# Heads' states multiplied turned round in a hybrid decoder layer's mixer: ScalarE copies them, VectorE's work per head in another order

## The chip, the cores and the metric

The kernel runs on one core of a Trainium2 chip, in float32 for nearly everything. The metric is the device time in microseconds of one execution, as the median over several runs. The engines are TensorE (PE, with its weight loads PEld), VectorE (DVE), ScalarE (ACT), GpSimd (POOL) and SyncE (SP), which here only issues transfers.

## The reference

One inference step of a decoder layer over 512 prompt tokens and 8 samples, width 1024: a mixer with a pooling part and an mLSTM part of 4 heads (128 wide), cross attention into 256 memory tokens, and a two-level mixture of 16 experts. The change lies in the mLSTM part. With no earlier state the prompt's heads come down to this, for each head:

```python
s   = einsum('bhjd,bhsd->bhjs', q, k) * w_intra          # causal scores
num = einsum('bhjs,bhsv->bhjv', s, v)
qn  = s.sum(-1)
h   = num / maximum(abs(qn), exp(-m_t))[..., None]
C_new = einsum('bhs,bhsv,bhsd->bhvd', w_state, v, k)     # an output, v rows by k columns
n_new = einsum('bhs,bhsd->bhd', w_state, k)              # an output
hn  = (h - mean(h)) * rsqrt(var(h) + eps)                # then times sigmoid(og) and a gain
```

The pooling part takes trailing means over 2, 4, 8 and 16 tokens minus the token itself, and multiplies each of its four channel groups by a 128 x 128 matrix. Both parts together go through one output projection.

## The kernel before

All five engines have an instruction list of their own, written out by hand; they meet through semaphores only. PSUM has two rings of three banks: one that ScalarE empties (`bank_a` on TensorE, `full` on ScalarE, counted by `act_full` and `act_free`) and one that VectorE empties (`bank_d`, `dve_full`, `dve_free`). A bank of a ring can be written again when the bank three before it in the ring's order has been taken.

Around the change TensorE does, for each head h of 0 to 3: `scores(h)` (four matmuls of 512, 384, 256 and 128 columns, L658, one bank each, and four transposes of the keys into a fifth bank, L663), then half of a projection (two channel blocks of `og` or `u`, L477, on ScalarE's ring), the transposes of the previous head (`transpose_heads`, L692), `numerators(h)` (ten matmuls of 129 columns, the 129th a column of ones that gives the sum, L673, ScalarE's ring), `state(h)` (L682 and L684) and the next head's scores. After `state(3)` come eight convolution matmuls of the pooling groups in the order 2, 3, 1, 0, each waiting for VectorE's `pool_diff` of its group (L738), then the first token tile's output projection (L774), in the midst of which stand the transposes of head 3.

VectorE does, for each head, `head_norm1(h)` (the denominator, the scaling of the numerators, `bn_stats` and `bn_aggr`), `take_state(h)` (two copies into `Cout`, L1910 and L1911), `products(h+1)` (scores times weights, L1877, and the keys times their state weights into `kw`, L1880), then work for the samples (`carried`, L1948), and `head_norm2(h)` (minus mean, times root, L1936). For head 2 `head_norm2` follows `products(3)` at once, and then come `pool_diff(2)`, `carried(4)`, `pool_diff(3)`, `carried(5)`, `take_heads(2)`, `take_last(0)`, `pool_diff(1)`, `pool_diff(0)` and `head_norm1(3)`. `pool_diff(0)` needs GpSimd's `window_sums`.

ScalarE copies the numerators (L1443) and then computes the next head's weights (`weights`, exponentials, L1434 and L1435), which the products need.

GpSimd takes the root of the variance (`head_rstd(h)`, which `head_norm2(h)` waits for), masks the products on the diagonal blocks (`masks(h)`, which `numerators(h)` waits for), brings the samples' states forward (`load_state`, `update_state`, each of these behind a `carried` of VectorE), and issues the states' stores (`state_out`).

`kw` and `Cout` lie in `gb`, the place of the norm vectors; the ln1 vectors are loaded there when all states are stored.

Of the kernel before, what the change touches and what calls it, by code (L numbers as in the profile page):

```python
# [18 lines left out]
ALU = mybir.AluOpType  # L19
ACT = mybir.ActivationFunctionType  # L20
# [106 lines left out]
def layer_kernel(nc, a, o):  # L127
# [3 lines left out]
    with ctx:  # L131
# [104 lines left out]
        kw = gb[:, 0, 0:512].rearrange("p (t k) -> p t k", t=NQT)  # L236
        Cout = gb[:, 1, 0:512].rearrange("p (b k) -> p b k", b=2)

# [93 lines left out]
        c_in = [sem(f"c_in{i}") for i in range(2)]  # L332
        c_store = [sem(f"c_store{i}") for i in range(2)]
        hs_var, hs_rstd = sem("hs_var"), sem("hs_rstd")
        sq2_out, kq_done = sem("sq2_out"), sem("kq_done")
# [113 lines left out]
        def _(pe):  # L449
# [227 lines left out]
            def state(h):  # L677

                pe.wait_ge(dve_free, at["keys", h])
                bk = bank_d()  # L680
                for i in range(NQT):
                    mm(bk[:, 0:HD], vn[:, i, h, 0:HD], kw[:, i, :], start=(i == 0), stop=(i == NQT - 1))  # L682
                for i in range(NQT):
                    last = mm(bk[0:1, HD:2 * HD], vn[:, i, h, HD:HD + 1], kw[:, i, :], start=(i == 0), stop=(i == NQT - 1))  # L684
                last.then_inc(dve_full, 1)
                at["state", h] = nd[0]

# [26 lines left out]
            at["og", 1] = na[0]  # L714
            transpose_heads(0)
            numerators(1)
            state(1)
# [3 lines left out]
            transpose_heads(1)  # L721
            transpose_last(1)
            numerators(2)
            state(2)
# [4 lines left out]
            at["heads", 2] = nd[0]  # L729
            transpose_last(0)  # L730
            numerators(3)
            state(3)
# [45 lines left out]
            for name, bk in zip(WO, banks):  # L778
                w = wring[:, BI[name] % WR]
                mm(bk[0:TR, :], mixT[:, KC - 1, 0:TR], w[:, KC - 1, :], start=False, stop=True).then_inc(dve_full, 1)  # L780
            rows_project(1, WO, mixT)
            transpose_x(0, x1_ready)
# [395 lines left out]
        def _(sp):  # L1178
# [41 lines left out]

            sp.wait_ge(act_full, at["pool"])
            for n in range(2):
                kv_load(n)
# [102 lines left out]
        def _(act):  # L1326
# [111 lines left out]
            def take_numerators(h):  # L1438
                if h >= 2:
                    act.wait_ge(dve_full, at["heads", h - 2])  # L1440
                for j in range(NQT):
                    bk = full()
                    A(hn[:, h % 2, j, :], bk[:, 0:HD + 1], ACT.Copy).then_inc(act_free, 1)  # L1443

            def take_og(cts):

                for ct in cts:
                    for c0, cn in GRP:
                        bk = full()
                        A(sgT[:, ct, c0:c0 + cn], bk[:, 0:cn], ACT.Exp, scale=-1.0).then_inc(act_free, 1)  # L1450
# [12 lines left out]
            take_og((0, 1))  # L1463
            take_numerators(0)
            weights(1)
            finish_og((0, 1))
            take_og((2, 3))
            take_numerators(1)
            weights(2)
            finish_og((2, 3))  # L1470
            take_projection(uT, (2, 3), 1.0, off=PADC)
            take_numerators(2)
            weights(3)
            take_projection(uT, (0, 1), 1.0, off=PADC)
            take_numerators(3)
            act.wait_ge(c_store[0], 16 * BUF.count(0))
            for g in (2, 3, 1, 0):
# [3 lines left out]
            def take_sample_rows(dstn):  # L1481
# [3 lines left out]
                last.then_inc(act_free, 1)  # L1485

            for t in range(3):
                take_x(t)
# [187 lines left out]
        def _(dve):  # L1676
# [228 lines left out]

            def take_state(h):
                bk = full()
                if h >= 2:
                    dve.wait_ge(c_out[h % 2], 32)
                V.tensor_copy(Cout[:, h % 2, 0:HD], bk[:, 0:HD])  # L1910
                V.tensor_copy(Cout[0:1, h % 2, HD:2 * HD], bk[0:1, HD:2 * HD]).then_inc(dve_free, 1)  # L1911

            def head_norm1(h):

                dve.wait_ge(act_free, at["numerators", h])
                x = hn[:, h % 2]
                qn = x[:, :, HD:HD + 1].rearrange("p t c -> p (t c)")
                d0 = den[:, 0, :]
                link(V.scalar_tensor_tensor(d0, qn, -1.0, qn, ALU.mult, ALU.max))
                fl = gcol[:, 16 + h:32:4]  # L1920
                link(V.tensor_tensor(d0, d0, fl, ALU.max))
                link(V.reciprocal(d0, d0))
                link(V.tensor_tensor(x[:, :, 0:HD], x[:, :, 0:HD], d0.unsqueeze(2).broadcast_to([128, NQT, HD]), ALU.mult))
                for t in range(NQT):
                    last = V.bn_stats(hst[:, t, :], x[:, t, 0:HD])
                link(last)
                for t in range(NQT):
                    last = V.bn_aggr(hagg[:, t, :], hst[:, t, :])
                last.then_inc(hs_var, 1)

            def head_norm2(h):
                dve.wait_ge(hs_rstd, h + 1)
                dve.wait_ge(hs_var, h + 1)
                for t in range(NQT):
                    x = hn[:, h % 2, t, 0:HD]
                    last = V.tensor_scalar(x, x, hagg[:, t, 0:1], den[:, 1, t:t + 1], ALU.subtract, ALU.mult)  # L1936
                last.then_inc(hn_ready, 1)
# [35 lines left out]

            head_norm1(0)
            take_state(0)
            products(1)
            carried(0)
            carried(1)
            head_norm2(0)
            take_heads(0)  # L1980
            head_norm1(1)
            take_state(1)
            products(2)
            carried(2)
            carried(3)
# [3 lines left out]
            head_norm1(2)  # L1989
            take_state(2)  # L1990
            products(3)
            head_norm2(2)
            pool_diff(2)
# [7 lines left out]
            head_norm1(3)  # L2001
            take_state(3)
            head_norm2(3)
# [465 lines left out]
        def _(pool):  # L2469
# [69 lines left out]
            def state_out(h):  # L2539
                pool.wait_ge(dve_free, at["state", h])  # L2540
                pool.dma_start(o_pC[0, 0, h], Cout[:, h % 2, 0:HD]).then_inc(c_out[h % 2], 16)
                pool.dma_start(o_pn[0, 0, h:h + 1], Cout[0:1, h % 2, HD:2 * HD]).then_inc(c_out[h % 2], 16)

# [59 lines left out]
            for h in (0, 1):  # L2603
# [3 lines left out]
                load_state(2 * h + 3)  # L2607
                state_out(h)
                head_rstd(h + 1, TR, NQT)
                masks(h + 2)  # L2610
            state_out(2)
            update_state(4)
            update_state(5)
            window_sums()
            load_state(6)
            head_rstd(3, TR, NQT)
            state_out(3)
            update_state(6)

            def norm_vectors(gname, bname):  # L2620
                pool.dma_start(gb[:, 0, :], a[gname][0].partition_broadcast(128)).then_inc(gb_in, 16)
                pool.dma_start(gb[:, 1, :], a[bname][0].partition_broadcast(128)).then_inc(gb_in, 16)


            for i in range(2):
                pool.wait_ge(c_out[i], 64)
            norm_vectors("ln1_g", "ln1_b")
            load_state(7)
# [3 lines left out]
            pool.dma_start(o_spool[0, :, 0:NPOOL - 1, :], a["cache_pool"][0, :, 1:NPOOL, :]).then_inc(un_out, 16)  # L2632
            norm_rstd(0)
            update_state(7)
            norm_rstd(1)
# [146 lines left out]
```

## Time and profile before

| what | value |
|---|---|
| median of 3 runs | 669.05 us (668.71 to 669.43) |
| profiled execution, its own time | 672.56 us |
| its span in the trace | 670.8 us |
| TensorE busy | 639.7 us (95%) |
| VectorE busy | 348.3 us (52%) |
| ScalarE busy | 151.8 us (23%) |
| GpSimd busy | 208.7 us (31%) |
| TensorE's part of the chain that ended last | 86% |

Times in the rows are microseconds from the span's start. In a timeline, equal neighbours are merged (x4 is four instructions), and the bracket at the end gives the idle time of the engine before them and what ended it. A float32 matmul leaves two records. "PE ps L682 x8" is eight records of line 682 writing PSUM. The line numbers are those of the kernel before.

### The profile page before, as it was taken

To read this page: it belongs to the slowest core of one execution; us is meant where nothing else is said; L and a number is where in the kernel's file an instruction comes from. 1 tells how busy PE (TensorE), PEld (TensorE's weight loads), DVE (VectorE), ACT (ScalarE), POOL (GpSimd) and SP (SyncE) were. 2 spreads that over 40 slices of the span, in tenths; PEclk is the share of its full clock that TensorE was granted. 3 is DMA by queue.
4 is the path that set the end of the run, shared out by engine and by line. 5 is a ranking of instruction groups with operands and counts; after the bars stand their busy time and mean duration, and the time that the engine had idled before them with its cause. 6 is when DMAs were issued, how large, how long until landed. Compare 5 with 4: busy or idle time off the path is not lost.

```text
span 670.8 us, 8667 instructions
## 1 busy us (share of the span) xinstructions
PE 639.7 (95%) x3244; PEld 392.0 (58%) x3244; DVE 348.3 (52%) x799; ACT 151.8 (23%) x333; POOL 208.7 (31%) x245
## 2 busy tenths in 40 slices
PE   6999999999999999999999899999899999999982
PEld 3445588887788774446888674444574454333330
DVE  0283356327456883757643856356863334253445
ACT  1113311102533230002002540223224111111144
POOL 4241010101566565412000985102344422111331
PEclk9999999999999999999999899999989999999996
DMA  8994478703353354004706777554539999999598
GB/s 301 391 319 165 142 172 225 250 20 126 99 171 116 102 201 149 17 0 148 291 0 245 256 268 301 220 178 168 235 124 385 410 414 404 373 354 412 196 204 161
DMA packets 45811, 146.14 MB, mean 218 GB/s; under 512 B 5738, under 2 KB 6058, under 8 KB 41663
## 3 DMA queue, kind: packets, MB, share of 16 engines
q1 hardware_dynamic: 31559, 107.50, 42.6%
q0 software_dynamic: 12032, 33.29, 17.6%
q10 hardware_dynamic: 2176, 4.76, 1.9%
q8 instruction: 27, 0.44, 0.3%
q14 instruction: 17, 0.14, 0.1%
HBM read 130.34 MB, written 20.33 MB: 225 GB/s over the span
## 4 chain that ended last, share of the span: by engine, by line
PE 86%; DMA 7%; DVE 2%; ACT 2%; POOL 1%; issue 1%; ACTq 0%; DVEq 0%; POOLq 0%
PE ps L602 14%; PE ps L749 13%; PE ps L1089 12%; PE ps L511 9%; PE ps L477 8%; PE ps L1109 5%; PE ps L600 4%; DMA xn<-y_d 3%; PE ps L850 2%; PE ps L774 2%; PE ps L976 2%; PE ps L658 2%; PE ps L1070 1%; PE ps L673 1%; PE ps L539 1%
## 5 line engine op out<-in xcount | busy, mean ns | idle before, releaser
L749 PE MATMUL ps<-wring,P 128*128 128x512 f32 x224 | 99.2, 596 | 0.0
L749 PEld LDWEIGHTS ps<-wring,P 128*128 128x128 f32 x224 | 41.6, 190 | 49.1 <-issue 49.0
L1089 PE MATMUL ps<-wring,P 128*32 128x512 f32 (+1 forms) x288 | 66.3, 604 | 0.9 <-DVE P L2344 0.9
L1768 DVE SCALAR_TENSOR_TENSOR P<-ps,P 128x264 f32<-128x264 f32 (+1 forms) x70 | 28.8, 426 | 61.0 <-PE ps L602 44.4
L511 PE MATMUL ps<-wring,P 128*128 128x512 f32 x128 | 58.2, 613 | 1.0 <-DVE P L1723 0.8
L477 PE MATMUL ps<-xT,wring 128*128 128x312 f32 (+1 forms) x256 | 56.8, 383 | 0.0
L2505 POOL TENSOR_SCALAR rstd<-agg 128x1 f32<-128x1 f32 (+1 forms) x15 | 16.8, 1120 | 113.5 <-DVE agg L1708 113.4
L477 PEld LDWEIGHTS ps<-xT,wring 128*128 128x128 f32 x256 | 46.6, 190 | 9.3
L2344 DVE COPY P<-ps 128x512 f32<-128x512 f32 x11 | 7.6, 691 | 76.7 <-PE ps L1070 71.2
L1089 PEld LDWEIGHTS ps<-wring,P 128*32 128x32 f32 (+1 forms) x288 | 22.6, 131 | 36.8 <-issue 36.8
L511 PEld LDWEIGHTS ps<-wring,P 128*128 128x128 f32 x128 | 24.7, 196 | 31.3 <-issue 31.0
L2650 POOL TENSOR_TENSOR P<-P,xT 128x2048 f32<-128x2048 f32 x8 | 36.0, 4520 | 11.9 <-DMA xT<-sq_d 9.1
L1109 PE MATMUL ps<-P 128*32 128x512 f32 (+1 forms) x144 | 32.6, 594 | 0.7 <-issue 0.7
L2020 DVE SCALAR_TENSOR_TENSOR xn<-xn,ps 128x512 f32<-128x512 f32 x16 | 10.9, 684 | 40.1 <-PE ps L749 28.1
L1368 ACT ACTIVATE xT<-ps 128x512 f32<-128x512 f32 (+1 forms) x30 | 13.9, 519 | 75.4 <-PE ps L539 75.2
L602 PE MATMUL ps<-xT,wring 128*128 128x264 f32 (+1 forms) x128 | 29.6, 387 | 0.0
L602 PE MATMUL ps<-P 128*128 128x264 f32 x128 | 29.5, 385 | 0.0
L602 PE MATMUL ps<-P,wring 128*128 128x256 f32 (+1 forms) x128 | 29.2, 382 | 0.0
L1089 PE MATMUL ps<-xT,P 128*32 128x512 f32 (+1 forms) x96 | 28.2, 593 | 0.0
L602 PEld LDWEIGHTS ps<-P 128*128 128x128 f32 x128 | 24.3, 190 | 4.2
L602 PEld LDWEIGHTS ps<-xT,wring 128*128 128x128 f32 x128 | 23.8, 190 | 4.8 <-issue 1.1
L602 PEld LDWEIGHTS ps<-P,wring 128*128 128x128 f32 x128 | 24.2, 190 | 3.8
(444 smaller groups left out, 1106.6 us busy)
## 6 DMA issues: line engine op xcount, KB each, us to landing
wring<-in_w_in SPq DMA_DIRECT2D x5, 2048.0 KB, 10.2
wring<-in_w_gate SPq DMA_DIRECT2D x10, 1024.0 KB
wring<-in_w_up SPq DMA_DIRECT2D x10, 1024.0 KB
P<-in_w_down SPq DMA_DIRECT2D x10, 1024.0 KB, 11.7
P<-in_cache_mem_k SPq DMA_DIRECT2D x8, 1024.0 KB, 7.5
P<-in_cache_mem_v SPq DMA_DIRECT2D x8, 1024.0 KB, 4.9
y_d<-P POOLq DMA_DIRECT2D x1, 4160.0 KB, 32.3
wring<-in_ca_wv SPq DMA_DIRECT2D x2, 2048.0 KB, 19.9
```

Source lines behind the costliest of these rows:

```text
L477: last = mm(out, lhs(k), rhs(k), start=(k == 0), stop=(k == n - 1))
L511: last = mm(bk[:, :], memT[:, k, m * 128:m * 128 + 128], w[:, k, :], start=(k == 0), stop=(k == KC - 1))
L600: last = mm(bank[:, 0:n], x[:, k, 128 * i:128 * i + 128], w[:, k, :], start=(k == 0), stop=(k == 3))
L602: last = mm(bank[:, 0:n], w[:, k, 128 * i:128 * i + 128], x[:, k, :], start=(k == 0), stop=(k == 3))
L658: mm(bk[:, 0:NP_ - t * TR], kT[:, h, t * TR:t * TR + TR], qT[:, h, t * TR:NP_], start=True, stop=True).then_inc(dve_full, 1)
L749: last = mm(bk[:, :], src[:, k, START[t]:START[t] + TR], w[:, k, :], start=(k == 0), stop=(k == KC - 1))
L1089: last = mm(GU[p % 2][lo:lo + m, :].rearrange("p (g f) -> p g f", g=2), xgT[:, p % 3, k, lo:lo + m], gu[s][:, :, k, :], start=(k == 0), st ...
L1109: last = mm(YB[q][lo:lo + m, :], hT[:, p % 2, f, lo:lo + m], dn[s][:, f, q * 512:q * 512 + 512], start=(f == 0), stop=(f == 1))
L1368: A(xT[:, 4 * q:4 * q + 4, START[t]:START[t] + n], bk[:, 0:4 * n].rearrange("p (k c) -> p k c", k=4), ACT.Copy).then_inc(act_free, 1)
L1768: V.scalar_tensor_tensor(dst, src, scale, part, ALU.mult, ALU.add).then_inc(part_added, 1)
L2505: link(G.tensor_scalar(x, agg[0:n, 1:2], LN_EPS, None, ALU.add))
L2650: G.tensor_tensor(x, x, qb[:, b % 4:b % 4 + 1].broadcast_to([128, 2, D]), ALU.mult).then_inc(kq_done, 1)
```

## The change

- `state(h)` multiplies with the two operands exchanged. Each of four matmuls has `kw` as the weights and 129 columns of `vn` moving, so the bank holds the state with k on the partitions and v along the columns, and n as column 129. The second group of matmuls, with one row of output for n, is gone. The bank is now of ScalarE's ring.
- ScalarE takes it: `take_state(h)`, one copy of 128 columns and one of one column, behind `take_numerators(h)` and ahead of `weights(h+1)`. TensorE turns the copy back (`transpose_state(h)`, behind `transpose_heads(h)` and `transpose_last`; for head 3 in the output projection), and ScalarE copies the turned state (`take_turned_state(h)`). The places are three column ranges of `qT`, whose head is used up by then. `Cout` is gone.
- On VectorE `take_state` is gone, `head_norm1(h)` ends with the scaling, and the statistics are a step of their own, `head_statistics(h)`, behind `products(h+1)`.
- `head_norm2` uses `scalar_tensor_tensor` with the root broadcast along the columns as third operand, in place of `tensor_scalar` with the root as a second scalar.
- On GpSimd `state_out(h)` waits for ScalarE's turned copy, stands behind `head_rstd(h+1)` and `masks(h+2)`, and stores n as 128 pieces of 4 bytes; `state_out(2)` and `state_out(3)` come later, and the ln1 vectors are loaded earlier, as soon as TensorE has finished `state(3)`. SP waits for the states' stores before it loads the samples' memory keys, since they go over `qT`.

```diff
             def state(h):
                 pe.wait_ge(dve_free, at["keys", h])
-                bk = bank_d()
+                bk = bank_a()
                 for i in range(NQT):
-                    mm(bk[:, 0:HD], vn[:, i, h, 0:HD], kw[:, i, :], start=(i == 0), stop=(i == NQT - 1))
-                for i in range(NQT):
-                    last = mm(bk[0:1, HD:2 * HD], vn[:, i, h, HD:HD + 1], kw[:, i, :], start=(i == 0), stop=(i == NQT - 1))
-                last.then_inc(dve_full, 1)
-                at["state", h] = nd[0]
+                    last = mm(bk[:, 0:HD + 1], kw[:, i, :], vn[:, i, h, :], start=(i == 0), stop=(i == NQT - 1))
+                last.then_inc(act_full, 1)
+                at["state", h] = na[0]
+
+            def transpose_state(h):
+                pe.wait_ge(act_free, at["state", h])
+                nc.tensor.transpose(bank_a()[:, 0:HD], stateT[:, h, :], ident).then_inc(act_full, 1)
+                at["turned state", h] = na[0]
...
+            def take_state(h):
+                bk = full()
+                A(qT[:, h, 0:HD], bk[:, 0:HD], ACT.Copy)
+                A(state_n[:, h, :], bk[:, HD:HD + 1], ACT.Copy).then_inc(act_free, 1)
+
+            def take_turned_state(h):
+                bk = full()
+                A(stateC[:, h, :], bk[:, 0:HD], ACT.Copy).then_inc(act_free, 1)
...
             take_og((2, 3))
+            take_turned_state(0)
             take_numerators(1)
+            take_state(1)
             weights(2)
...
-                link(V.tensor_tensor(x[:, :, 0:HD], x[:, :, 0:HD], d0.unsqueeze(2).broadcast_to([128, NQT, HD]), ALU.mult))
+                V.tensor_tensor(x[:, :, 0:HD], x[:, :, 0:HD], d0.unsqueeze(2).broadcast_to([128, NQT, HD]), ALU.mult).then_inc(scaled_done, 1)
+
+            def head_statistics(h):
+
+                x = hn[:, h % 2]
+                dve.wait_ge(scaled_done, h + 1)
...
-                    last = V.tensor_scalar(x, x, hagg[:, t, 0:1], den[:, 1, t:t + 1], ALU.subtract, ALU.mult)
+                    last = V.scalar_tensor_tensor(x, x, hagg[:, t, 0:1], den[:, 1, t:t + 1].broadcast_to([128, HD]), ALU.subtract, ALU.mult)
...
             head_norm1(2)
-            take_state(2)
             products(3)
+            head_statistics(2)
             head_norm2(2)
             pool_diff(2)
...
                 load_state(2 * h + 2)
                 load_state(2 * h + 3)
-                state_out(h)
                 head_rstd(h + 1, TR, NQT)
                 masks(h + 2)
-            state_out(2)
+                state_out(h)
...
             window_sums()
+            pool.wait_ge(act_full, at["state", 3])
+            norm_vectors("ln1_g", "ln1_b")
             load_state(6)
+            state_out(2)
             head_rstd(3, TR, NQT)
-            state_out(3)
             update_state(6)
-            for i in range(2):
-                pool.wait_ge(c_out[i], 64)
-            norm_vectors("ln1_g", "ln1_b")
...
             norm_rstd(0)
+            state_out(3)
             update_state(7)
```

## Rows read from the trace of the kernel before

**Rows 1.** The page's slices: busy tenths of TensorE in 40 equal slices.
```profile
PE   6999999999999999999999899999899999999982
```

**Rows 2.** Windows: start:end, width, busy us of each engine, granted clock, DMA share, GB/s.
```profile
220.00:240.00 20.00, 20.00 (x101) 15.52 (x100) 18.35 (x61) 4.12 (x14) 10.47 (x15) 1.00 0.23 71
376.00:384.00 8.00, 7.34 (x31) 5.97 (x32) 7.33 (x19) 4.39 (x15) 8.00 (x3) 0.79 0.75 251
```

**Rows 3.** Chain that ended last, around heads 2 and 3: start, us, what.
```profile
219.71 0.89 PE ps L682 x8
220.60 0.96 PE ps L684 x8
221.57 2.62 PE ps L658 x8
224.18 0.63 PE ps L663 x4
...
238.84 0.44 PE ps L692 x4
...
246.80 1.14 PE ps L738 x4
247.94 6.01 PE ps L774 x14
```

**Rows 4.** Waits of TensorE's weight loads, 155 to 262 us: total us, times, longest.
```profile
PEld ps L658 <- DVE gb L1911: 1.4, 3, 0.5
PEld ps L658 <- DVE P L1877: 1.1, 4, 0.3
...
PEld ps L738 <- DVE P L1972: 0.5, 2, 0.3
```

**Rows 5.** VectorE's timeline, 220 to 247 us: start, us, line, operation [idle before].
```profile
220.67 0.69 DVE L1923 TENSOR_TENSOR P<-P,den 128x512 f32<-128x512 f32 x1
221.40 0.87 DVE L1925 BATCH_NORM_STATS2 hst<-P 128x6 f32<-128x128 f32 x4
222.30 0.38 DVE L1928 BATCH_NORM_AGGREGATE hagg<-hst 128x2 f32<-128x6 f32 x4
...
224.85 1.13 DVE L1880 TENSOR_SCALAR gb<-ps,wcol 128x128 f32<-128x128 f32 x4 [0.22 <-PE ps L663]
...
226.92 2.14 DVE L441 TENSOR_TENSOR P<-P 128x512 f32<-128x512 f32 x3
...
239.32 0.75 DVE L1942 SCALAR_TENSOR_TENSOR P<-ps,colv,P 128x512 f32<-128x512 f32 x1 [0.82 <-PE ps L692]
...
240.32 2.54 DVE L441 TENSOR_TENSOR P<-P 128x512 f32<-128x512 f32 x2
...
245.50 0.17 DVE L1968 TENSOR_TENSOR P<-P,con 128x16 f32<-128x16 f32 x1
...
246.66 0.16 DVE L1919 SCALAR_TENSOR_TENSOR den<-P 128x4 f32<-128x4 f32 x1
```

**Rows 6.** VectorE's timeline, the scaling of head_norm2 and what precedes head 3's.
```profile
185.28 4.51 DVE L1936 TENSOR_SCALAR P<-P,hagg,den 128x128 f32<-128x128 f32 x4
...
248.90 0.38 DVE L1928 BATCH_NORM_AGGREGATE hagg<-hst 128x2 f32<-128x6 f32 x4
...
250.77 1.12 DVE L1936 TENSOR_SCALAR P<-P,hagg,den 128x128 f32<-128x128 f32 x4 [1.13 <-POOL den L2537]
```

**Rows 7.** GpSimd's timeline, 242 to 248 us.
```profile
242.60 0.80 POOL L2561 DMA_DIRECT2D out<-P  x1 [0.29 <-POOL P L2559]
243.42 1.05 POOL L2565 TENSOR_TENSOR P<-P 128x512 f32<-128x512 f32 x1
247.74 0.77 POOL L2548 DMA_DIRECT2D P<-in_state_mlstm_C  x1 [3.27 <-DMA out<-P]
```

**Rows 8.** ScalarE's timeline after head 2's numerators.
```profile
219.92 0.29 ACT L1434 ACTIVATE wcol<-P,gcol 128x1 f32<-128x1 f32 x1
220.11 0.71 ACT L1435 ACTIVATE P<-P,gcol 128x512 f32<-128x512 f32 x1
```

More of the change, by code:

```diff
@@ L236, in layer_kernel @@
         kw = gb[:, 0, 0:512].rearrange("p (t k) -> p t k", t=NQT)
-        Cout = gb[:, 1, 0:512].rearrange("p (b k) -> p b k", b=2)
+        stateT, stateC, state_n = qT[:, :, 0:HD], qT[:, :, HD:2 * HD], qT[:, :, 2 * HD:2 * HD + 1]
         kvr = view(0, 6144, "p (s m d) -> p s m d", s=3, m=2)
@@ L333, in layer_kernel @@
         c_store = [sem(f"c_store{i}") for i in range(2)]
+        scaled_done = sem("scaled_done")
         hs_var, hs_rstd = sem("hs_var"), sem("hs_rstd")
@@ L715, in _ @@
             transpose_heads(0)
+            transpose_state(0)
             numerators(1)
@@ L722, in _ @@
             transpose_last(1)
+            transpose_state(1)
             numerators(2)
@@ L730, in _ @@
             transpose_last(0)
+            transpose_state(2)
             numerators(3)
@@ L780, in _ @@
                 mm(bk[0:TR, :], mixT[:, KC - 1, 0:TR], w[:, KC - 1, :], start=False, stop=True).then_inc(dve_full, 1)
+            transpose_state(3)
             rows_project(1, WO, mixT)
@@ L1221, in _ @@
             sp.wait_ge(act_full, at["pool"])
+            for i in range(2):
+                sp.wait_ge(c_out[i], 64)
             for n in range(2):
@@ L1464, in _ @@
             take_numerators(0)
+            take_state(0)
             weights(1)
@@ L1471, in _ @@
             take_projection(uT, (2, 3), 1.0, off=PADC)
+            take_turned_state(1)
             take_numerators(2)
+            take_state(2)
             weights(3)
             take_projection(uT, (0, 1), 1.0, off=PADC)
+            take_turned_state(2)
             take_numerators(3)
+            take_state(3)
             act.wait_ge(c_store[0], 16 * BUF.count(0))
@@ L1485, in take_sample_rows @@
                 last.then_inc(act_free, 1)
+            take_turned_state(3)
             for t in range(3):
@@ L1904, in _ @@
             link(V.tensor_tensor(v4(vsn), v4(vsn), b4(sg8[:, 32:36]), ALU.mult))
[L1906 to L1911, printed above, removed]
             def head_norm1(h):
@@ L1974, in _ @@
             head_norm1(0)
-            take_state(0)
             products(1)
+            head_statistics(0)
             carried(0)
@@ L1981, in _ @@
             head_norm1(1)
-            take_state(1)
             products(2)
+            head_statistics(1)
             carried(2)
@@ L2001, in _ @@
             head_norm1(3)
-            take_state(3)
+            head_statistics(3)
             head_norm2(3)
@@ L2539, in state_out @@
             def state_out(h):
-                pool.wait_ge(dve_free, at["state", h])
-                pool.dma_start(o_pC[0, 0, h], Cout[:, h % 2, 0:HD]).then_inc(c_out[h % 2], 16)
-                pool.dma_start(o_pn[0, 0, h:h + 1], Cout[0:1, h % 2, HD:2 * HD]).then_inc(c_out[h % 2], 16)
+                pool.wait_ge(act_free, at["turned state", h])
+                pool.dma_start(o_pC[0, 0, h], stateC[:, h, :]).then_inc(c_out[h % 2], 16)
+                pool.dma_start(o_pn[0, 0, h].rearrange("(k one) -> k one", one=1), state_n[:, h, :]).then_inc(c_out[h % 2], 16)
             def load_state(b):
@@ L2607, in _, with norm_vectors @@
                 load_state(2 * h + 3)
-                state_out(h)
                 head_rstd(h + 1, TR, NQT)
                 masks(h + 2)
-            state_out(2)
+                state_out(h)
+            def norm_vectors(gname, bname):
+                pool.dma_start(gb[:, 0, :], a[gname][0].partition_broadcast(128)).then_inc(gb_in, 16)
+                pool.dma_start(gb[:, 1, :], a[bname][0].partition_broadcast(128)).then_inc(gb_in, 16)
             update_state(4)
@@ L2614, in _ @@
             window_sums()
+            pool.wait_ge(act_full, at["state", 3])
+            norm_vectors("ln1_g", "ln1_b")
             load_state(6)
+            state_out(2)
             head_rstd(3, TR, NQT)
-            state_out(3)
             update_state(6)
-            def norm_vectors(gname, bname):
-                pool.dma_start(gb[:, 0, :], a[gname][0].partition_broadcast(128)).then_inc(gb_in, 16)
-                pool.dma_start(gb[:, 1, :], a[bname][0].partition_broadcast(128)).then_inc(gb_in, 16)
-            for i in range(2):
-                pool.wait_ge(c_out[i], 64)
-            norm_vectors("ln1_g", "ln1_b")
             load_state(7)
```

## The prediction

> **What bounds the kernel now.** I read the page's slices first, then windows, then the chain that ended last in the stretch of the change, then what TensorE's weight loads waited for, and last the three other engines' timelines over one head. In the slices TensorE is at nine tenths or more from the second to the 22nd, some 17 to 369 us [rows 1]; in 220 to 240 us it is busy 20.00 of 20.00 us at full clock, VectorE 18.35, ScalarE 4.12 [rows 2]. The chain there runs through TensorE alone [rows 3]. So an instruction taken from TensorE is worth its length, up to the next place where TensorE waits, and those places are what matters. The weight loads' waits show two: the scores (1.4 us in three times for the state copies, L1911, and 1.1 us in four for the products, L1877), and the pooling convolutions, L738, which waited twice for pool_diff (L1972), 0.5 us together [rows 4]. The second is small, but it says that VectorE's chain up to pool_diff(0) has no slack. I work out both sides of that place.
>
> **TensorE's saving.** A state costs 0.89 us for the 128-column outer products and 0.96 us for the one-row ones [rows 3]. The new form needs one group of four matmuls of 129 columns, again 0.89 us. So 0.96 us goes in each of four heads. A turned state is one transpose; four took 0.44 us [rows 3], so 0.11 us each comes back.
>
> **The stall in the scores.** From the start of the scores to that of the keys is 2.61 us [rows 3]; their 512 + 384 + 256 + 128 = 1280 columns at the state's rate (0.89 us for 512) are 2.2, and the keys' four transposes take 0.63 against 0.44 for four others: 0.6 us of stall. Before, the next head's first product stood behind statistics that ended at 222.68 and two state copies, 1.4 us or so after the scores began at 221.57 [rows 3, 5]. Now it stands only behind the scaling, which ended at 221.36 [rows 5]. But it also needs ScalarE's weights, and these now stand behind take_state, which waits for TensorE's state. Weights started 0.21 us after the numerators ended (219.92 against 219.71), and small ScalarE instructions follow each other by 0.19 us [rows 3, 8]. With the state ending at 220.60 and one copy more, weights start at 221.00, 1.08 us later than they did, and the first exponential ends at 220.11 + 0.71 + 1.08 = 221.90 [rows 8]. The new scores begin at 220.60, so the first product starts 1.35 us after them, against 1.4. The stall stays; with this little a head gives about 0.98 us. Bounds on the stall: it grows by as much as it could shrink, 0.3 us, or vanishes, 0.55 us.
>
> Before head 2's numerators end, that is 2 x 0.98 - 2 x 0.11 = **1.74 us** gained. From here all times are on the old trace's clock, set by the end of head 2's numerators (219.71).
>
> **VectorE's chain to the convolutions.** Before, head_norm2(2) followed products(3) without a pause, since GpSimd's root had run under them. Now head_statistics(2) stands behind products(3), and head_norm2(2) right behind it, so nothing covers the root. The keys' scaling ended at 224.85 + 1.13 = 225.98 and now ends at 225.0. Statistics take 222.68 - 221.40 = 1.28 us [rows 5], to 226.3. The root costs what head 3 shows, where it lies bare: aggregation ended at 248.90 + 0.38 = 249.28, head_norm2 started at 250.77, 1.49 us [rows 6]: 227.8. Then head_norm2. No row has the three-operand form on 128 x 128; the nearest, the same operation over 512 columns, took 0.75 us [rows 5], which for four short ones is a lower bound; undisturbed the plain form took 1.12 us for the four [rows 6], and I take that (bounds 0.75, and 1.5 with GpSimd's masks(3) beside it). pool_diff(2) then starts at 228.9, not at 226.92 [rows 5]: **1.9 us late**, and everything up to carried(5) with it.
>
> VectorE had 0.82 us of idle time before take_heads(2) [rows 5], so pool_diff(1) starts 1.1 us late, at 241.4. From there to the end of pool_diff(0) was 246.66 - 240.32 = 6.34 us [rows 5]: 247.7. On the other side, GpSimd's update_state(5) waits for carried(5), and window_sums behind it feeds pool_diff(0): 243.42 + 1.05 + 1.9 = 246.4 [rows 7], plus 246.66 - 245.50 = 1.16 us for pool_diff(0) [rows 5]: 247.6. Both answers agree. pool_diff(1) may meet one more of update_state(5)'s three operations: two adds took 2.54 us there, where three took 2.14 undisturbed [rows 5]. I take 248.0, bounds 247.2 and 248.5. That is 1.35 us later than 246.66. TensorE would be ready for the last group 0.98 + 0.96 - 0.11 = 1.8 us before its undisturbed 246.3, at 244.5, so it waits over 3 us, and the whole of state(3)'s saving goes there: the convolutions end **1.35 us** late on this clock.
>
> The scaling's four plain forms took 4.51 us beside update_state and 1.12 without it [rows 6]. The Trainium skill (SBUF — State Buffer, Who interferes with whom) says that VectorE and GpSimd block each other when VectorE runs in a two-port mode, and also when it reads two SBUF inputs against a GpSimd operation that reads SBUF; the first half agrees with those rows, and the second speaks against the new form, whose broadcast den is a second input. By it the new form is still delayed, if by less. The sum is the same by either, since heads 0 and 1 have slack: the heads' transposes come 14 us after the keys (224.8 to 238.84 [rows 3]), and 4.51 us fitted in there.
>
> **Moves at no cost.** take_state's VectorE copies are counted above. The ln1 vectors come earlier. The state stores move behind the masks, which puts update_state(2) and load_state(4), (5) later; carried(4) takes these only after pool_diff(2). SP's new wait for the stores stands behind the load of wc0, which itself waits for the samples' output projection, later in TensorE's order than the last state. The stores of n become 128 pieces of 4 bytes, beside other work; if that cover went, they would cost one short transfer. transpose_state(3) adds **0.11 us** in the output projection.
>
> **Sum.** -1.74 + 1.35 + 0.11 = -0.3 us. The profiled execution took 672.56 us, its span 670.8; the median of the runs is 669.05. The terms are shifts along one chain, so I take them off the median: 668.75, **668.7 us**. Behind the convolutions TensorE is again full [rows 1], and the transfers it meets later start from its own progress, so a shift passes through.
>
> **Rivals.**
> - *The saving reaches the end.* VectorE's chain is shorter than I read it, by contention gone. Then 4 x 0.96 - 4 x 0.11 = 3.4 us: 665.6. Against it: TensorE waits at L738 even today [rows 4]. Chance 0.08.
> - *The stall in the scores vanishes*, if ScalarE's copies don't hold the weights up. 3 x 0.55 us more, since head 2's part moves VectorE's chain too: -0.3 - 1.65 = -2.0, 667.1. Chance 0.12.
> - *GpSimd is late with head 3's root; slower.* In front of head_rstd(3) now stand the ln1 loads, load_state(6) and state_out(2). load_state(6) waits for update_state(5)'s store, issued at 242.60 and landed at 247.74 [rows 7]; 1.9 us later is 249.6. Four issues of at most 0.8 us [rows 7], some 2.6, give 252.2; root 1.49, scaling 1.12: 254.8. TensorE wants the heads 6.01 us behind the convolutions' end at 247.94 + 1.35 [rows 3], at 255.3. So it decides from 0.5 us more on; a store 3 us later gives -0.3 + 2.5 = +2.2, 671.2. Chance 0.07.
> - *The clock falls.* After TensorE's waits for the samples' queries it was granted 0.79 over 376 to 384 us [rows 2], 1.2 GHz in part and 2.4 in the rest: 8 x 0.21 = 1.7 us. Behind the wait before L738 that makes -0.3 + 1.7 = +1.4: 670.4. Against it: this wait is far shorter than that one. Chance 0.09.
> - *My forecast*, 0.61; the rest, 0.03, on both sides.
>
> The Trainium skill (TensorE: Matmul & The Clock Gate, Part 1) says that the gate halves TensorE's clock once it has been idle; the row at 376 us agrees. By the page this rival would be likelier than I give it.
>
> **Numbers.** A measurement of this kernel tells about 0.2%, 1.34 us, from no change. My own case alone spans 668.0 to 669.6. Low end 667.0: the stall gone. High end 670.6: pool_diff(0) at 248.5 with the clock fallen, or the heads of 3 a little late. Left out are the first rival and the worst of the third. Faster 0.20: the first two rivals; slower 0.15: the last two, less their mild forms; same 0.65.
>
> **What would show it.** Keys that start 3.5 us after the numerators, not 4.47; an idle of 1.5 us before head_norm2(2); weight loads of L738's successor waiting some 3 us for pool_diff. If that wait is missing, VectorE's chain is misread, and the time is near 665.6. If TensorE waits for hn_ready(3), the third rival holds.

## The result, and the profile after

The changed kernel takes 672.99 us (median of 20 runs, 667.67 to 678.02) against 669.82 for the kernel before (20 runs, 668.42 to 670.98): ratio 1.0037, 95% interval 1.0021 to 1.0053. It is slower, by 2.5 us in the ratio, where it was forecast 0.3 us faster, and its times now spread over 8.5 us where they spread over 2.6. (The ratio and this spread leave out one disturbed run, that of 678.02 us.) The profiled execution took 670.82 us, its span 669.1; so this one profile shows less of the loss than a typical execution has. The line numbers of the changed kernel are a few to some 30 higher: L738 is L745, L658 is L659, L692 is L696, L1877 is L1904, L1936 is L1961, L1972 is L1997, L2561 is L2586.

What was forecast for a head is there. The chain around head 1 (start, us, what):

```profile
176.03 0.89 PE ps L683 x8
176.92 1.95 PE ps L659 x6
...
179.49 0.67 PE ps L664 x4
```

The keys start 3.46 us after the numerators end, 4.47 before [rows 3]; the one-row group is gone and the stall in the scores is not. VectorE's timeline behind head 2 (start, us, line, operation, bracket the idle time before and its releaser):

```profile
224.87 0.38 DVE L1953 BATCH_NORM_AGGREGATE hagg<-hst 128x2 f32<-128x6 f32 x4
226.74 1.26 DVE L1961 SCALAR_TENSOR_TENSOR P<-P,hagg,den 128x128 f32<-128x128 f32 x4 [1.48 <-POOL den L2562]
227.92 2.13 DVE L442 TENSOR_TENSOR P<-P 128x512 f32<-128x512 f32 x3
...
246.05 0.17 DVE L1997 SCALAR_TENSOR_TENSOR P<-csum,P 128x8 f32<-128x8 f32 x1
...
247.29 0.16 DVE L1939 SCALAR_TENSOR_TENSOR den<-P 128x4 f32<-128x4 f32 x1
```

The root lies bare for 1.48 us, and pool_diff(2) starts 227.92 - 218.78 = 9.14 us behind the end of head 2's numerators, where it was 226.92 - 219.71 = 7.21 [rows 3, 5]: 1.93 us late, as forecast. New is how TensorE and ScalarE fare at the convolutions. First the windows (start:end, width, busy us of the engines, granted clock, DMA share, GB/s), then TensorE's timeline, then ScalarE's:

```profile
220.00:240.00 20.00, 19.86 (x104) 16.17 (x103) 17.52 (x55) 5.25 (x17) 11.84 (x17) 1.00 0.34 99
240.00:250.00 10.00, 7.18 (x28) 5.02 (x27) 9.53 (x26) 4.12 (x11) 8.91 (x11) 0.83 0.91 305
```

```profile
240.85 1.57 PE L745 MATMUL ps<-P,poolw 128*128 128x312 f32 x6
244.97 1.03 PE L745 MATMUL ps<-P,poolw 128*128 128x208 f32 x2 [2.55 <-ACT P L1506]
246.27 3.08 PE L745 MATMUL ps<-P,poolw 128*128 128x312 f32 x8 [0.27 <-DVE P L1997]
```

```profile
244.40 1.26 ACT L1506 ACTIVATE P<-ps,colv 128x312 f32<-128x312 f32 x3 [3.00 <-DMA out<-P]
```

ScalarE empties TensorE's banks at L1506 into a place from which GpSimd's store of a sample's state is still leaving. That store was issued at 237.10; ScalarE was let go at 244.40. In the same stretch SP issued a 2 MB load (the cross attention's query weights) at 236.96, when TensorE had used up the block before. GpSimd's row and SP's:

```profile
237.10 0.82 POOL L2586 DMA_DIRECT2D out<-P  x1 [0.29 <-POOL P L2584]
```

```profile
236.96 0.37 SPq L1190 DMA_DIRECT2D wring<-in_ca_wq  x1
```

Before, the store stood at 236.11 and the load at 238.88, 2.8 us behind it; TensorE's lead brought the load forward, by 2.3 us against the first head's scores, and VectorE's delay put the store back by 0.6, and they met. TensorE then idled 2.55 us, the granted clock over 240 to 250 us is 0.83 where windows of full clock had been, so 1.2 GHz in part, and the last eight records took 3.08 us.

A second delay came from head 1, where I had seen slack. The chain, 193 to 216 us:

```profile
193.80 5.22 DMA out<-P
...
200.04 7.48 DMA P<-qk_d
...
210.96 4.53 DVE P L1961 x4
...
215.54 0.66 PE ps L696 x4
```

Another store, issued at 193.80 beside SP's 2 MB load at 194.21, landed late; load_state(3) waits for it, carried(3) for that load, and norm2(1) stands behind carried(3). TensorE waited 0.7 us for the scaled heads before it could transpose them. Its weight loads' waits, 155 to 262 us (total us, times, longest):

```profile
PEld ps L659 <- DVE P L1904: 1.6, 4, 0.5
...
PEld ps L745 <- ACT P L1506: 3.0, 1, 3.0
...
PEld ps L745 <- DVE P L1997: 0.8, 1, 0.8
PEld ps L696 <- DVE P L1961: 0.7, 1, 0.7
```

### The profile page after: what moved, and what is told of

Its sections match the earlier page's. It is cut to its first block, busy times and chain, and to the rows that moved or that the text cites. A ratio compares the mean times of both kernels' runs of the same rounds, so it can differ in the third digit from the quotient of the medians.

```text
span 669.1 us, 8617 instructions
## 1 busy us (share of the span) xinstructions
PE 634.8 (95%) x3216; PEld 389.3 (58%) x3216; DVE 344.5 (51%) x791; ACT 154.2 (23%) x345; POOL 209.0 (31%) x245
## 4 chain that ended last, share of the span: by engine, by line
PE 76%; DMA 9%; DVE 8%; POOL 3%; ACT 2%; issue 1%; ACTq 0%; DVEq 0%; POOLq 0%
PE ps L603 14%; PE ps L756 14%; PE ps L1097 12%; PE ps L512 9%; PE ps L1117 5%; PE ps L601 4%; DMA xn<-y_d 3%; PE ps L478 2%; PE ps L858 2%; PE ps L781 2%; PE ps L984 1%; PE ps L1078 1%; DVE P L442 1%; PE ps L540 1%; DMA P<-qk_d 1%
```

## The experiments

Each was timed beside the kernel before on the same chip, and the ratio is to that. "Out" is where TensorE starts the output projection, in us after the start of the first head's scores in its one profile; "clock" is the granted clock over 240 to 250 us there. The kernel before has a median of 671.6 us on the chip of the four kernels from "statistics of head 2 first" to "before, matmuls added", and of 669.5 to 670.0 on the others; so kernels are compared by their ratios and not by their medians. Each row has twelve runs, but "before" and "after" have 20, "before, late statistics" six and "statistics of heads 0, 1 first" seven.

| kernel | median us | ratio (95% interval) | out | clock |
|---|---|---|---|---|
| before | 669.82 | | 91.6 | 1.00 |
| after | 672.99 | 1.0037 (1.0021 to 1.0053) | 92.6 | 0.83 |
| statistics first | 670.16 | 1.0002 (0.9985 to 1.0020) | 90.7 | 1.00 |
| plain scaling | 673.03 | 1.0043 (1.0026 to 1.0060) | 93.2 | 0.77 |
| root covered for head 2 | 670.44 | 1.0009 (0.9986 to 1.0031) | 91.7 | 0.83 |
| wq0 load held back | 673.50 | 1.0052 (1.0032 to 1.0073) | 92.8 | 0.83 |
| wait filled | 671.75 | 1.0026 (1.0008 to 1.0043) | 91.9 | 1.00 |
| head 1 scaled before carried(3) | 672.24 | 1.0039 (1.0016 to 1.0063) | 92.5 | 0.83 |
| chain shortened | 669.69 | 0.9999 (0.9981 to 1.0016) | 89.3 | 1.00 |
| before, late statistics | 672.86 | 1.0047 (1.0030 to 1.0065) | 94.7 | 0.88 |
| statistics of head 2 first | 671.19 | 0.9995 (0.9968 to 1.0023) | 90.3 | 1.00 |
| statistics of heads 0, 1 first | 676.07 | 1.0080 (1.0052 to 1.0109) | 94.2 | 0.78 |
| before again | 670.46 | 0.9994 (0.9972 to 1.0015) | 91.6 | 1.00 |
| before, matmuls added | 672.89 | 1.0026 (1.0002 to 1.0049) | 93.8 | 1.00 |
| shortest chain | 669.58 | 0.9996 (0.9969 to 1.0023) | 89.4 | 1.00 |
| chain shortened again | 671.08 | 1.0017 (0.9997 to 1.0038) | 89.3 | 1.00 |

**Statistics first.** For heads 0, 1 and 2 of the changed kernel:

```diff
-            products(h+1)
             head_statistics(h)
+            products(h+1)
```

> The changed kernel with the statistics of head 0, 1 and 2 back ahead of the next products. Theory A (the statistics behind products(3) lay GpSimd's root bare and make VectorE, and with it the samples' stores, late; TensorE then idles before the convolutions and its clock falls there): the root is covered again, pool_diff(2) starts about 1.9 us earlier, the wait of ScalarE's L1506 for the store (3.0 us) is gone, no wait for head 1's scaled heads, no fall of the clock near 245 us; the scores stall 0.8 us more per head. Convolutions end near 247.5 us in the trace, median 0 to 1 us below the kernel before. Theory B (the loss of the median comes from falls of the clock later on, which the order of the heads' work doesn't touch): median as that of the changed kernel, 2 to 3 us above before.

The whole loss is gone. The store is issued at 234.80 and SP's load at 237.55, the order of before, and no row of ScalarE waiting for a store is left. The stall in the scores grows instead:

```profile
PEld ps L659 <- DVE P L1904: 3.8, 4, 1.2
...
PEld ps L745 <- DVE P L1997: 1.6, 2, 1.2
```

**Plain scaling.** `scalar_tensor_tensor` back to `tensor_scalar` with the root as second scalar.

> The changed kernel with the plain two-scalar scaling (tensor_scalar) in head_norm2. Theory A: nothing on the chain but head 1's scaling, which takes 4.5 us in either form beside update_state, and head 2's, 1.1 instead of 1.26: within 0.5 us of the changed kernel. Theory C (the three-operand form itself costs by contention with GpSimd's reads): 0.5 to 1 us less than the changed kernel.

Nothing comes back that these intervals can show; the three-operand form doesn't carry the loss.

**Root covered for head 2.**

```diff
-            head_norm2(2)
             pool_diff(2)
+            head_norm2(2)
```

> The changed kernel with head_norm2(2) behind pool_diff(2), so that GpSimd's root of head 2 runs under it. Theory A: everything from pool_diff(2) to carried(5) 1.5 us earlier, the store of update_state(4) issued at 235.6 and not 237.1, before the 2 MB load of wq0 at about 236.8, landing within 3 us; the 3.0 us wait of ScalarE is gone, convolutions end 1.5 us earlier or more, no fall of the clock there. Median 2 to 3 us below the changed kernel. Theory B: 0 to 1.5 us below it.

0.9 us of "out" and most of the median come back, though its profile still shows a fallen clock there, behind a wait of 2.3 us for pool_diff (`PEld` of L745). Its interval excludes neither no loss nor 0.3%, and the profiled execution, at 676.45 us, is the longest of its twelve.

**wq0 load held back.** SP waits for the store before this one block.

```diff
+                if i == BI["wq0"]:
+                    sp.wait_ge(c_store[0], 16 * BUF.count(0))
                 block_load(i)
```

> The changed kernel with SP's load of wq0 held until the stores of the states in buffer 0 have landed; nothing else moves. Theory A: the store of update_state(4) lands within 3 us of its issue, ScalarE's 3.0 us wait is gone; TensorE still waits for pool_diff until 246.1. So the clock there decides: if it stays at 2.4 GHz the convolutions end at 248.2 instead of 249.35 and the median falls 1 to 2 us; if it falls all the same, under 0.5 us. Theory B: no difference.

ScalarE's wait for the store is gone and nothing is won: TensorE now waits as long for pool_diff, 4.1 us in two, and the clock falls all the same.

```profile
PEld ps L745 <- DVE P L1999: 4.1, 2, 3.8
```

So the collision was one of two waits that end close to each other; VectorE's chain stands right behind it.

**Wait filled with matmuls.** Six matmuls of 256 columns whose result nothing reads, one ahead of the third pooling group and five in the second.

> The changed kernel with six matmuls of 256 columns into an unused bank (0.43 us each, 2.6 us in all) where TensorE stands idle in the convolutions: five ahead of the fourth, one ahead of the wait for the third group's pool_diff. They add work and take no wait away. Theory A1 (the idle time makes the clock fall there, and this fall is most of the loss): no fall near 245 us, the convolutions' end 1.3 us earlier although TensorE does more, the median 1.5 to 3 us below the changed kernel and its runs closer together. Theory A2 (the late chain itself is the loss, the clock an accident): the median of the changed kernel, within 0.7 us, or more by what the fillers delay.

The clock over 240 to 250 us is 1.00 again and "out" is 0.7 us earlier than in the changed kernel, with TensorE doing some 2.6 us more work in the stretch. So the profile shows the clock's part. The runs do not settle it: 1.0026 against 1.0037 would be about a third of the loss, but the two intervals overlap over most of their length.

**Head 1 scaled before carried(3).**

```diff
-            carried(3)
             head_norm2(1)
+            carried(3)
```

> The changed kernel with carried(3) behind head_norm2(1) on VectorE. In the changed kernel carried(3) waited 3.2 us for a transfer behind the 2 MB load of wo1, and TensorE then waited 0.7 us for head 1's scaled heads. Expected: that wait gone, head 2's numerators 0.6 us earlier; but the convolutions still wait for VectorE's and GpSimd's chain, which shifts with head 2, while load_state(4) and (5) come with the same delay. Median 0.3 to 0.8 us below the changed kernel by theory A; by theory B (later falls of the clock carry the loss) no difference.

The 0.7 us wait for head 1's scaled heads goes, and scores(3) start at 62.47 instead of 62.92 us after scores(0). ScalarE's wait for the store takes it all (`PEld` of L745 on L1506 3.8 us).

**Chain shortened.** The two edits above (norm2(2) behind pool_diff(2), carried(3) behind norm2(1)), and GpSimd's `window_sums()` ahead of `update_state(5)`.

> The changed kernel with three moves: head_norm2(2) behind pool_diff(2), carried(3) behind head_norm2(1), and GpSimd's window_sums ahead of update_state(5), in the gap where it waits for carried(5). If the chain to pool_diff(0) is what the change ran into, the convolutions now end about 2.5 to 3 us earlier than in the changed kernel, TensorE's idle time before them is under 1 us, the clock stays, and the median is 2.5 to 4 us below the changed kernel, 0 to 1.5 us below the kernel before. By theory B it is no better than the kernel before by more than noise, with wide spread.

"Out" is 2.2 us earlier than before, and the time is level (at most 1.3 us shorter by the interval). Where those 2.2 us go is the last question below.

**Before, late statistics.** The kernel before, with the statistics a step of their own behind the next products, and nothing else of the change.

> The kernel before with one part of the change alone: the statistics of heads 0 to 2 behind the next head's products, everything else as it was. The root of head 2 lies bare (1.5 us), VectorE's chain to pool_diff(0) is 1.5 to 2.5 us later, and TensorE, which is not faster here, waits 1 to 2 us for it in the convolutions. Theory A: 1 to 2 us above the kernel before, with a fall of the clock in some executions. Theory B: equal to the kernel before.

This one edit, made for all the heads, makes a loss as large as the change's. The same row of ScalarE waiting for a store appears, and TensorE waits behind it:

```profile
ACT P L1481 <- DMA out<-P: 5.1, 1, 5.1
PEld ps L739 <- ACT P L1481: 3.2, 2, 3.0
```

The store is issued at 238.04 us and SP's load at 238.03. TensorE has a small lead here too, 0.8 us at that load against the first head's scores: with the statistics behind, the products wait for nothing of VectorE's but the scaling.

**Statistics of head 2 first**, and **of heads 0 and 1 first**: the diff of the first experiment for that head or those heads alone.

> The changed kernel with the statistics back ahead of the next products for head 2 alone; heads 0 and 1 keep them behind. Theory A (it is head 2's moved statistics, with GpSimd's root bare behind them, that make VectorE, GpSimd and then the convolutions late): the wait before the convolutions is short, the clock stays at 1.00 there, and the median is level with the kernel before, 670.2 against about 669.9 us, like the run with all three undone; the output projection starts near 91 us after the first head's scores. Rival B (each of the three moves adds its share, by head 1's scaled heads coming late and by the scores): only a third to a half of the loss goes, 671.5 to 672 us, and head 1's wait of 0.7 us before its transposes stays.

> The reverse: statistics back ahead of the products for heads 0 and 1, behind them for head 2 alone. Theory A: the loss stays, 672.5 us or more, with VectorE or a store's landing as what ScalarE and the weight loads wait for before the convolutions, and a granted clock under 1.00 in the windows from 240 to 250 us. Rival B: half of the loss goes, 671.3 us.

Head 2 alone takes the loss away, and heads 0 and 1 alone don't; they make it larger, since the stall in the scores grows again (3.1 us of waiting for the products, against 1.6 in the changed kernel) and VectorE's late chain stays. On one chip the two kernels differ by 0.85% in their ratios, 0.7% in their medians. TensorE at the convolutions, first with head 2's statistics first, then with them behind:

```profile
241.14 1.98 PE L745 MATMUL ps<-P,poolw 128*128 128x312 f32 x8
244.49 2.30 PE L745 MATMUL ps<-P,poolw 128*128 128x312 f32 x8 [1.37 <-DVE P L1997]
```

```profile
241.93 1.57 PE L745 MATMUL ps<-P,poolw 128*128 128x312 f32 x6
245.53 1.06 PE L745 MATMUL ps<-P,poolw 128*128 128x208 f32 x2 [2.03 <-ACT P L1506]
247.36 3.83 PE L745 MATMUL ps<-P,poolw 128*128 128x312 f32 x8 [0.77 <-DVE P L1997]
```

An idle of 1.37 us leaves the clock at 1.00 and the last eight records at 2.30 us; idles of 2.03 and 0.77 us are followed by 3.83.

**Before again, and with matmuls added.** The first is the kernel before unchanged. The second has five matmuls of 256 columns ahead of its last convolution matmuls.

> The kernel before, unchanged, under another label: how far two sets of runs of one kernel lie apart, and a second profile of it. Expected: ratio 1.000, its interval within 0.15% on either side. For the last transfer of a sample's memory values, which took 6.6 us in the one profile of before and 8 to 10 us in four of the eight experiments: if the new order has nothing to do with it, a second profile of before may show 8 us as well; if 6.6 again, that stays open.

> The kernel before with five matmuls of 256 columns, whose result nothing reads, ahead of the last convolution matmuls: TensorE works some 2.2 us more there and idles no more than before, so everything behind is shifted by that. If a shift passes through to the end, the median is 2.2 us up, 672.1 us. If something later has its own time and takes a shift in (as the run with the shortened chain suggests, which was 2.2 us earlier here and level at the end), it is under 1 us up. With no idle the clock stays at 1.00 at the convolutions, so a rise by 3 us or more would mean that extra work costs as much as the same time idle, and that the clock explains little of the loss.

Two sets of runs of one kernel lie 0.06% apart, with an interval of 0.2% on either side; so less than that is not told here. The added work moves "out" by 2.2 us and the time by 0.26%, 1.7 us, with an interval from 0.1 to 3.3. That agrees with a shift that passes through; it excludes a shift that vanishes, if by little.

**Shortest chain, and chain shortened again.** The first has head 2's statistics ahead of the products, norm2(1) ahead of carried(3) and window_sums ahead of update_state(5). The second repeats the chain shortened.

> The changed kernel with head 2's statistics back ahead of the products, head_norm2(1) ahead of carried(3), and window_sums ahead of update_state(5): the combination that should be the fastest up to the output projection. Theory A: no wait over 1 us before the convolutions, the output projection starts near 88.8 us after the first head's scores (91.6 before), so 2.8 us earlier. If that passes through to the end as the added matmuls did, the ratio is 0.996. If something later takes it in, as for the shortened chain, it is 0.998 to 1.001, and the profile shows a longer wait for the last transfer of memory values near 440 us, or a clock below 1.00 in the windows from 440 to 460 us.

> The kernel of the shortened chain, unchanged, on this chip and with a second profile: whether its gain of 2.2 us up to the output projection is again not in the median (ratio 0.998 to 1.001), and whether the last transfer of memory values again takes 8 us where the kernel before showed 6.6, 6.9 and 6.9. If it takes 6.6 here and the ratio is 0.997, the missing gain was chance of those runs.

Both reach the output projection 2.2 us before the kernel before does, and neither is shown to end earlier. (The interval of the first still has room for 2.1 us; those of the two sets of the second have room for 1.3 and 0.2.) The chain names the same place in all: the transfer of the last sample's memory values, 1 MB, which is issued as soon as its place is free. Before again, shortest chain and chain shortened again, in this order:

```profile
442.74 6.89 DMA P<-in_cache_mem_v
```

```profile
441.08 8.20 DMA P<-in_cache_mem_v
```

```profile
441.12 7.79 DMA P<-in_cache_mem_v
```

Against the first head's scores it starts 2.4 us earlier in the short chains and lands 1.1 and 1.5 us earlier, since it takes 1.3 and 0.9 us longer. TensorE's timeline of the shortest chain, with its windows, shows what follows:

```profile
449.32 1.11 PE L905 MATMUL ps<-P 128*32 128x256 f32 x16 [2.24 <-DMA P<-in_cache_mem_v]
450.37 5.30 PE L756 MATMUL ps<-wring,P 128*128 128x512 f32 x8
```

```profile
450.00:460.00 10.00, 10.00 (x43) 4.16 (x39) 3.62 (x7) 0.95 (x6) 1.88 (x2) 0.83 0.83 315
```

TensorE idles 2.24 us there, 0.64 and 0.93 in the two profiles of the kernel before, and then eight records take 5.30 us at a clock partly fallen, against 3.70 at full clock. In the three profiles of the two short chains that is 0.9 to 1.6 us of waiting more and 1.6 to 1.7 us of clock: in these executions the lead of 2.2 us is used up.

## Why the prediction was wrong, step by step

- **TensorE's saving: right.** Forecast 3 x 0.98 - 2 x 0.11 = 2.7 us up to scores(3). Without head 1's wait it was 65.30 - 62.47 = 2.8; with it 2.4.
- **The stall in the scores: right.** It stays, 1.6 us in four for the products, and its cause is the one worked out, ScalarE's weights. VectorE's first product of head 3 waits for them and starts 1.43 us behind the scores (219.51), where I had 1.35:

```profile
220.94 2.04 DVE L1904 TENSOR_TENSOR P<-ps,P 128x512 f32<-128x512 f32 x4 [0.51 <-ACT P L1445]
```


- **VectorE's chain: right.** pool_diff(2) 1.93 us late (forecast 1.9), the root bare for 1.48 (1.49). pool_diff(0) ended 247.29 - 218.78 = 28.5 us behind the numerators, on the old clock 248.2, where I had 248.0 within 247.2 and 248.5. The scaling took 1.26 us, inside its bounds.
- **"Heads 0 and 1 have slack": wrong, small.** I held the 4.5 us of scaling against 14 us of room and left out what stands ahead of it: a store beside a 2 MB load, the load behind that store, and carried(3). It cost 0.45 us, a term that the sum doesn't have.
- **"The convolutions end 1.35 us late": this step failed.** I let TensorE wait for pool_diff and go on at full clock. Against the scores' start the output projection was to begin 0.4 us earlier than before; it began 1.0 us later. Head 1 is 0.45 of the difference, pool_diff(0) 0.2. The rest, 0.8, is the clock: four records behind pool_diff(0) at 1.14 us [rows 3] would have ended at 248.5, and they ended at 249.35. That is 1.4 us of the 2.8 between my -0.3 and the +2.5 of the ratio.
- **The rival "the clock falls": it held.** I priced it at 1.7 us; it is 0.8 in the changed kernel's profile and 1.4 to 1.7 in those of plain scaling, root covered, wq0 held back, head 1 scaled first, and heads 0 and 1 first. I gave it 0.09 because the wait was "far shorter" than that before 376 us [rows 2]. 2.55 us of idle was enough; in the profiles here idles of 1.97 us and more at this place were followed by a fallen clock, and those of 1.41 us and less were not. The Trainium skill (TensorE: Matmul & The Clock Gate, Part 1) has an idle TensorE fall to half its clock; these rows agree in that the granted clock is down to 0.83, and I should have priced the idle that my own sum had made, "over 3 us", as that case and not as a rival.
- **A wait that no step had.** The store of update_state(4) against SP's load of wq0. I moved GpSimd's chain by 1.9 us and TensorE's by as much the other way, and did not look at what of the two shares the 16 DMA engines. The Trainium skill (DMA: Bandwidth & Descriptors, SWDGE vs HWDGE vs iDMA) says that GpSimd's and SP's queues are served in turn inside each DMA engine; the store's 7.3 us to its release beside the load agrees with that. But holding the load back won nothing, since pool_diff stood right behind: the last eight records of the convolutions start 89.7 us after the first head's scores with the load held back and without. This wait is one face of the loss, not its cause.
- **The cause.** The moved statistics of head 2. Undoing the move for head 2 alone brings "out" from 92.6 to 90.3 us and the ratio from 1.0037 to 0.9995, and undoing it for heads 0 and 1 alone does neither (94.2, 1.0080). In the kernel before, the same move for all heads loses 1.0047; head 2's alone was not run there. The forecast had the mechanism, and its size up to pool_diff(0). But with it undone the change is level, and not faster by its lead at the output projection; so a second part of the loss stands behind that place.
- **The sum has only 0.11 us behind the convolutions: this failed too, and its cause is open.** The change ends 2.5 us later and "out" is 1.0 later, so some 1.5 us lie elsewhere. The table says more, as an estimate: take the shift of "out" from the loss that the ratio gives. For the three further sets of runs with the old form of the states (late statistics, before again, matmuls added) that leaves 0.0, -0.4 and -0.4 us. For the twelve sets with the new form it leaves 0.4 to 3.4 us, 1.7 in the mean, as much with a lead as with a delay. Each such value is uncertain by 1 to 2 us, since "out" is from one profile and the ratio has its interval; but all twelve lie on one side. So shifts at the output projection do reach the end, as I had it, and the new form costs some 1.7 us that my sum doesn't have, in the main behind that place. With the statistics back in their place the lead of 0.9 us goes into that (1.0002).
- **GpSimd late with head 3's root: it did not hold.** The transposes of head 3 follow the first part of the output projection without a wait, 6.01 us behind its start, as before.

How much of the 2.5 us comes from which place in a typical execution is only in part shown. The profile shows 1.0 us at the output projection, and its own time is 2.2 us under the median. Much of the difference between executions goes with the clock: of the changed kernel's runs the five up to 670.2 us had a mean granted clock of 0.989 to 0.991 over the span, the eight from 674.0 to 676.2 us one of 0.980 to 0.986; 0.007 of 670 is 4.7 us, and the two groups are some 5 to 6 us apart. But where in the span it falls in the long ones is not shown. It need not be at the convolutions: statistics of head 2 first and shortest chain, whose clock stood at 1.00 there in their profiles, spread over 9 to 10 us too. The profile of the first is of its longest execution, 676.31 us, and has its fall behind the transfer of the memory values:

```profile
449.88 1.94 PE L905 MATMUL ps<-P 128*32 128x256 f32 x16 [2.65 <-DMA P<-in_cache_mem_v]
```

```profile
450.00:460.00 10.00, 10.00 (x33) 4.15 (x34) 2.64 (x7) 0.95 (x6) 0.58 (x1) 0.69 0.70 272
```

That of root covered for head 2, 676.45 us, shows the same: 2.92 us of idle there and a granted clock of 0.66.

**Open** is the transfer of memory values. It took 7.8 to 10.3 us in eight of twelve profiles with the new form of the states (the changed kernel's own, with 6.62, is not among the eight) and 6.6 to 6.9 in all four with the old. Four of the eight (plain scaling, root covered for head 2, head 1 scaled before carried(3), statistics of heads 0 and 1 first) had no lead at the output projection, and statistics first, with a lead of 0.9 us, took 6.61. So a lead alone doesn't explain it. It may be that something in the new form (the states' stores at other times, for one) delays this transfer whatever the lead; or, with so few profiles, chance. No run here tells these apart. The busy tenths of the 16 DMA engines in 40 slices from 438 to 452 us, first of the kernel before again, then of the shortest chain, show only how it ends:

```profile
DMA  0200000000000092959999999999999999200009
```

```profile
DMA  0000001009909999998889999999932111000090
```

In the second the last 1.1 us of the transfer, to 449.28 us, show a busy share of one to three tenths. If the new form delays it, that may be the 1.7 us, or a part of them.

## What to carry to other kernels

Where the sum makes TensorE idle, the clock's price belongs in the sum and not among the rivals: here some 2 to 3.5 us of idle cost 0.8 to 1.7 us more behind it. When one engine's chain is put back and another's brought forward, list the transfers that each issues, for they may now meet. A saving far ahead of the end is not yet a saving at the end: set the shift at a fixed place beside the shift of the whole time, for every variant. What is left over, with a lead as with a delay, is a cost that the sum does not have, and the next waits for a transfer are where to look for it.

## What was not expected of the hardware

- GpSimd's store of a state issued 0.14 us behind SP's 2 MB load let ScalarE go 7.3 us after its issue. Issued 2.8 us ahead of the load, as in the kernel before, it held nobody up.
- 2.55 us of idle were followed by a granted clock of 0.83 over 10 us; 1.37 us were not. Each of these is one execution; whether the fall comes in every one is not shown.
- The three-operand form beside GpSimd's update_state took 4.53 us for four tiles (the chain above), as the plain form did (4.51, [rows 6]). The Trainium skill (SBUF — State Buffer, Who interferes with whom) says so of an instruction with two SBUF inputs; I had expected it to be delayed less.
- One and the same 1 MB load took from 6.5 to 10.3 us over sixteen profiles, with the kernel's other work ordered almost alike.
